# A transformer block's first MLP: block products by seven half-size ones, and one completion signal per weight unit

## The reference

```python
def squared_relu_mlp(h, w_in, w_out):
    return jnp.square(jax.nn.relu(h @ w_in)) @ w_out      # w_in 1024 x 4096, w_out 4096 x 1024
...
xl = xl + ml[5] * squared_relu_mlp(modulate(xl, norm_mlp_g[i], ml[3], ml[4]), w_mlp_in[i], w_mlp_out[i])
xc = xc + mc[5] * squared_relu_mlp(modulate(xc, norm_mlp_g[i], mc[3], mc[4]), w_mlp_in[i], w_mlp_out[i])
```

## Time and profile before

| what | value |
| --- | --- |
| median of 3 runs | 1614.97 us (1614.3 to 1968.04) |
| span of the profiled execution, first to last instruction | 1613.1 us |
| its instructions | 24225 |
| matmuls | 9440 |
| granted TensorE clock, 40 slices | nine tenths or more in each |
| HBM traffic | 100 GB/s over the span |

### The profile page before, as it was taken

One profiled execution on the slowest core, in us unless ns is written; L12 is line 12 of the kernel. 1 busy time (PEld: TensorE's weight loads), 2 busy tenths in 40 slices (PEclk: granted clock), 3 DMA queues, 4 the chain that ended last, 5 costly groups with the idle time before them and its releaser, 6 DMA issues.

```text
span 1613.1 us, 24225 instructions
## 1 busy us (share of the span) xinstructions
PE 1595.3 (99%) x9440; PEld 1433.7 (89%) x9440; DVE 983.8 (61%) x1315; ACT 517.5 (32%) x931; POOL 618.0 (38%) x402
## 2 busy tenths in 40 slices
PE   8999999999999999999999999999999999999998
PEld 5889988989999999999999888878889888888887
DVE  5697457258756764865784678229975825344364
ACT  4422466233211211211211512138864422222222
POOL 2422565335323322432331544244505644444441
PEclk9999999999999999999999999999999999999999
DMA  9473212213252234223332122110002322323221
GB/s 361 181 284 134 92 41 99 92 66 105 77 185 80 77 122 140 100 95 117 105 112 97 66 91 92 65 56 1 1 1 89 107 93 92 104 91 99 96 79 53
DMA packets 50334, 162.99 MB, mean 101 GB/s; under 512 B 6336, under 2 KB 8768, under 8 KB 46656
## 3 DMA queue, kind: packets, MB, share of 16 engines
q1 hardware_dynamic: 50240, 161.68, 29.1%
HBM read 158.78 MB, written 2.10 MB: 100 GB/s over the span
## 4 chain that ended last, share of the span: by engine, by line
PE 93%; DVE 3%; DMA 2%; issue 1%; ACT 1%; SPq 0%; POOL 0%; POOLq 0%; DVEq 0%; ACTq 0%
PE ps L1714 26%; PE ps L1715 26%; PE ps L1716 26%; PE ps L2259 3%; PE ps L2221 2%; PE ps L2248 1%; PE ps L2126 1%; PE ps L2114 1%; PE ps L2154 1%; PE ps L1938 1%; DMA mod_late<-w_mod_dram 1%; DMA mod_big<-w_mod_dram 1%; DVE h L1315 1%; DMA raw<-units_dram 1%; PE ps L2149 1%
## 5 line engine op out<-in xcount | busy, mean ns | idle before, releaser
L625 POOL TENSOR_TENSOR w_lo<-raw,w_hi 128x1024 fp32r<-128x1024 f32 (+1 forms) x235 | 483.6, 2070 | 837.9 <-ACT w_hi L784 837.7
L1714 PE MATMUL ps<-h,w_hi 128*128 128x384 f32 (+2 forms) x1176 | 409.8, 348 | 1.7 <-DVE h L1315 1.2
L1715 PE MATMUL ps<-h,w_lo 128*128 128x384 f32 (+2 forms) x1176 | 407.6, 347 | 0.0
L1716 PE MATMUL ps<-h,w_hi 128*128 128x384 f32 (+2 forms) x1176 | 407.3, 346 | 0.0
L784 ACT ACTIVATE w_hi<-raw 128x1024 fp32r<-128x1024 f32 x187 | 197.8, 1058 | 372.7 <-PE ps L1716 366.1
L1714 PE MATMUL ps<-hid_lo,w_hi 128*128 128x384 f32 (+2 forms) x800 | 277.6, 347 | 0.0
L1715 PE MATMUL ps<-hid_hi,w_lo 128*128 128x384 f32 (+2 forms) x800 | 276.6, 346 | 0.0
L1716 PE MATMUL ps<-hid_hi,w_hi 128*128 128x384 f32 (+2 forms) x800 | 276.4, 346 | 0.0
L1714 PEld LDWEIGHTS ps<-h,w_hi 128*128 128x128 f32 x1176 | 221.3, 188 | 25.2 <-issue 3.4
L1716 PEld LDWEIGHTS ps<-h,w_hi 128*128 128x128 f32 x1176 | 221.2, 188 | 16.4
L1715 PEld LDWEIGHTS ps<-h,w_lo 128*128 128x128 f32 x1176 | 221.4, 188 | 16.0
(11 more groups left out here) (237 smaller groups left out, 2268.9 us busy)
## 6 DMA issues: line engine op xcount, KB each, us to landing
raw<-units_dram SPq DMA_DIRECT2D x187, 512.0 KB, 3.3
mod_ring<-w_mod_dram SPq DMA_DIRECT2D x96, 256.0 KB, 3.3
mod_big<-w_mod_dram SPq DMA_DIRECT2D x16, 1024.0 KB, 10.2
mod_late<-w_mod_dram SPq DMA_DIRECT2D x8, 1024.0 KB, 7.9
xl<-x_dram SPq DMA_DIRECT2D x2, 2048.0 KB, 8.4
bias<-bias_dram SPq DMA_DIRECT2D x8, 384.0 KB, 3.7
xc<-ctx_dram SPq DMA_DIRECT2D x2, 1024.0 KB, 10.5
out_dram<-out_t SPq DMA_DIRECT2D x16, 128.0 KB, 1.9
```

What stands on the lines that cost most here:

```text
L625: ins = nc.gpsimd.tensor_tensor(w_lo[:, s, sl], raw[:, s, sl], w_hi[:, s, sl].bitcast(F32), op=ALU.subtract)
L1714: mm(out, a[0], b[1], start=start, stop=False)
L1715: mm(out, a[1], b[0], start=False, stop=False)
L1716: return mm(out, a[0], b[0], start=False, stop=stop)
```

## The change

The first MLP is cut into eight blocks (0 to 7) of 512 hidden columns. Block 0 does its first matrix as before (four units). In blocks 1 to 7 the product of a 1024 x 512 weight block and h is seen as a 2 x 2 matrix of halves (512 rows or 256 columns of the weights, 384 tokens), and computed with seven products of halves, 24 matmuls each, in place of eight (the Strassen-Winograd form). For it:

- four combinations of halves of h are made once, in block 0, by VectorE (`difference`, `less`, then `turn_high` on ScalarE and `turn_low` on VectorE): t1 replaces a quarter of h, t2, t3 and t4 are new tiles of 128 x 1536;
- four sums of weight quarters are made per block by GpSimd, so a block has four raw units but seven split ones in the first matrix;
- three of the four results are joined: ScalarE copies a partial product out of PSUM (`copy`), later products go on top of it in the same bank, and VectorE adds the copy (`joined`). The relu of three quarters is inside VectorE's square. The high part of the hidden layer is made by ScalarE, `quarter_high`.

The second matrix of blocks 0 to 5 has units of 512 x 256: two output tiles and four k-tiles each, in four banks (4 to 7), with one `unit_done` for both tiles, and every block adds all eight output tiles to the residual. Blocks 6 and 7 share one second matrix with whole units, as before. The chunks of `w_mod` are spread anew, up to two a block, and all loops of this stage are written out. The second layer's MLP is unchanged but for names. The core of the diff:

```diff
+BLOCKS = 8
+MOD_SEQ = [12, 16, 13, 17, 14, 18, 15, 19, 20, 21, 22, 23]
+MOD_OF = {b: [2 * b - 2, 2 * b - 1] for b in range(1, 6)} | {6: [10], 7: [11]}
...
+            for b in range(1, BLOCKS):
+                r, cs = M0 + block_raw(b) + 4, MOD_OF[b]
+                load_unit(r)
+                load_mod(cs[0], (4, 5))
+                load_unit(r + 1)
+                load_mod(cs[0], (6, 7))
+                load_unit(r + 2)
+                load_unit(r + 3)
...
+                    def outer_sums():
+                        raw_here(1)
+                        raw_here(3)
+                        if b == 1:
+                            pool.wait_ge(t_lo, 4)
+                        else:
+                            pool.wait_ge(lo_made, M0 + block_first(b - 1) + 4)
+                        nc.gpsimd.tensor_tensor(w_sum[:], a21, a22, op=ALU.add).then_inc(w_sums, 1)
+                        raw_here(0)
+                        pool.wait_ge(w_sums, n + 1)
+                        nc.gpsimd.tensor_tensor(a21, a11, a21, op=ALU.subtract).then_inc(w_sums, 1)
+
+                    if b < 7:
+                        outer_sums()
+                    low(w)
+                    if b == 7:
+                        outer_sums()
+                    pool.wait_ge(w_sums, n + 2)
+                    pool.wait_ge(lo_made, w + 1)
+                    nc.gpsimd.tensor_tensor(a11, w_sum[:], a11, op=ALU.subtract).then_inc(w_sums, 1)
+                    low(w + 1)
+                    raw_here(2)
+                    pool.wait_ge(w_sums, n + 3)
+                    pool.wait_ge(lo_made, w + 2)
+                    nc.gpsimd.tensor_tensor(w_sum[:], a12, a11, op=ALU.subtract).then_inc(w_sums, 1)
+                    for j in range(2, 11 if b < 6 else 7):
+                        low(w + j)
...
+                for i in range(4):
+                    u = M0 + i
+                    act.wait_ge(unit_done, u + 1)
+                    for bank, c0, n in both if i < 3 else even:
+                        ins = nc.scalar.activation(hidl_f[:, i, c0:c0 + n], ps[:, 2 * pair_of(u, i, True) + bank, 0:n],
+                                                   ACT.Relu)
+                    ins.then_inc(relu0_made, 1)
+                    high_u(u + 4)
+                    act.wait_ge(sq0_made, i + 1)
+                    nc.scalar.activation(hidh[:, i], hidl_f[:, i], ACT.Copy).then_inc(hq_hi, 1)
+                    if i == 1:
+                        turn_high(0, t3h[:], t3f[:])
+                    elif i == 2:
+                        turn_high(1, t2h[:], t2f[:])
+                        turn_high(2, t4h[:], t4f[:])
+                act.wait_ge(unit_done, M0 + 4)
+                turn_high(3, h_hi[:, 0:4, H1], t1f[:])
...
+                    high_sum(b, 3)
+                    copy(0, 0, 2)
+                    high_sum(b, 4)
+                    copy(1, 1, 1)
+                    high_u(w + 5)
+                    copy(0, 2, 0)
+                    high_u(w + 6)
+                    for q in range(4):
+                        if q == 3:
+                            copy(0, 6, 3, ACT.Relu)
+                        if b == 6 and q in (1, 2):
+                            high_sum(7, q)
+                        elif b != 6 or q == 0:
+                            high_u(w + 7 + q)
+                        quarter_high(q)
...
+                def difference(dst, spare, j0, tok0, j1, tok1):
+                    tt(dst, half_f(j0, 0, tok0), half_f(j1, 0, tok1), op=ALU.subtract).then_inc(dsteps, 1)
+                    st.n = st.n + 1
+                    st.wait(tt(spare, half_f(j0, 1, tok0), half_f(j1, 1, tok1), op=ALU.subtract))
+                    tt(dst, dst, spare, op=ALU.add).then_inc(tf_made, 1)
+
+                def less(dst, src, n, j, tok):
+                    dve.wait_ge(tf_made, n)
+                    st.wait(tt(dst, half_f(j, 0, tok), src, op=ALU.subtract))
+                    tt(dst, dst, half_f(j, 1, tok), op=ALU.add).then_inc(tf_made, 1)
...
+                difference(t1f[:], t4f[:], 0, H1, 0, H0)
+                first_square(0)
+                dve.wait_ge(tf_made, 1)
+                difference(t3f[:], t4f[:], 1, H1, 0, H1)
+                first_low(0)
+                less(t2f[:], t1f[:], 1, 1, H1)
+                first_square(1)
+                less(t4f[:], t2f[:], 3, 1, H0)
+                first_low(1)
+                turn_low(0, t3l[:], t3f[:], t3h[:])
+                first_square(2)
+                first_low(2)
+                turn_low(1, t2l[:], t2f[:], t2h[:])
+                turn_low(2, t4l[:], t4f[:], t4h[:])
+                first_square(3)
+                first_low(3)
+                turn_low(3, h_lo[:, 0:4, H1], t1f[:], h_hi[:, 0:4, H1])
...
+                def add_tile(b, m):
+                    w = M0 + block_first(b) + (7 if b else 4) + m // 2
+                    dve.wait_ge(unit_done, w + 1)
+                    add_pieces(0, 2 + m % 2, m, 5, xa(0, b, m))
...
+                    def joined(side, p, q):
+                        dve.wait_ge(unit_done, M0 + block_first(b) + p + 1)
+                        dve.wait_ge(s_copied, 4 * (b - 1) + (3, 2, 1)[q])
+                        src = quarter(b, q)[2]
+                        tt(src, part_ps(b, side), src, op=ALU.add).then_inc(s_added, 1)
+                        dve.wait_ge(s_added, 3 * (b - 1) + q + 1)
+                        square(q, 4 * b + q, src)
...
+                    steps(c, range(6))
+                    joined(1, 3, 0)
+                    steps(c, range(6, 7))
+                    low(0)
+                    joined(0, 4, 1)
+                    steps(c, range(7, 8))
+                    low(1)
+                    if b == 6:
+                        extract_late(c, 4)
+                    joined(1, 5, 2)
+                    low(2)
+                    dve.wait_ge(s_copied, 4 * b)
+                    square(3, 4 * b + 3, quarter(b, 3)[2])
+                    low(3)
+                    if b < 6:
+                        add_tile(b, 0)
+                        add_tile(b, 1)
+                        extract_late(c, 0)
+                        for m in range(2, 6):
+                            steps(c + 1, range(2 * m - 4, 2 * m - 2))
+                            add_tile(b, m)
+                        add_tile(b, 6)
+                        extract_late(c + 1, 0)
+                        add_tile(b, 7)
...
+                def second(b, before_tile):
+                    for n in range(4):
+                        u = M0 + block_first(b) + (7 if b else 4) + n
+                        s = u % SLOTS
+                        pe.wait_ge(lo_made, u + 1)
+                        for m, c in ((0, 1), (1, 1), (0, 0), (1, 0)) if n == 0 else ((0, 0), (0, 1), (1, 0), (1, 1)):
+                            tile = 2 * n + m
+                            if c == (n == 0):
+                                before_tile(tile)
+                            for k in range(4):
+                                if n == 0 and m == 0 and b == 0 and c:
+                                    pe.wait_ge(hq_made, k + 1)
+                                elif n == 0 and m == 0 and b and k % 2 == 0:
+                                    pe.wait_ge(hq_made, 4 * b + (1 if c else 3) + k // 2)
+                                w = slice(512 * m + P * k, 512 * m + P * k + P)
+                                cols = (H0, H1)[c]
+                                ins = three(ps[:, 4 + 2 * m + c, 0:EVEN], (w_hi[:, s, w], w_lo[:, s, w]),
+                                            (hidh[:, k, cols], hidl[:, k, cols]), k == 0, k == 3)
+                        ins.then_inc(unit_done, 1)
+
+                def before_second(b):
+                    def wait(tile):
+                        if b == 0 and tile == 0:
+                            pe.wait_ge(relu0_made, 4)
+                        elif b or tile > 1:
+                            pe.wait_ge(x_added, xa(0, b, tile) - 1)
+                        if tile == 2 and b:
+                            mod_mm(MOD_OF[b][0], 0)
+                        if tile == 7 and b:
+                            mod_mm(MOD_OF[b][1], 0)
+                    return wait
...
+                def product(b, p):
+                    u = M0 + block_first(b) + p
+                    s, bank = u % SLOTS, 2 * (p % 2) + (4 if b == 7 else 0)
+                    pe.wait_ge(lo_made, u + 1)
+                    if p in (2, 3, 4):
+                        pe.wait_ge(s_copied, 4 * (b - 1) + p - 1)
+                    elif p in (5, 6):
+                        pe.wait_ge(s_added, 3 * (b - 1) + p - 4)
+                    for m in range(2):
+                        for k in range(4):
+                            w = slice(512 * m + P * k, 512 * m + P * k + P)
+                            ins = three(ps[:, bank + m, 0:EVEN], (w_hi[:, s, w], w_lo[:, s, w]), operands[p](k),
+                                        k == 0 and p in (0, 1, 5), k == 3, onto=p in (2, 3, 4, 6))
```

(17 more changed lines are left out.)

435 lines of the change are left out of this document (300 added, 135 removed).

## The result

The changed kernel took 1766.1 us (median of 4 runs, 1753.1 to 1769.1) beside 1614.8 for the kernel before on the same chip (median of 4, one of which took 1968.04 us for a reason that is not known): a ratio of 1.092, interval 1.088 to 1.096. It is slower, as forecast, but by 151 us where 107 were forecast, and beyond the upper end of the range, 1752.

The account below looks back on a forecast made before the run. TensorE was taken to bound the kernel. A gain of 29.1 us from fewer matmuls against losses of 29.7, 27, 44, 15, 4 and 16 gave +106.6: 1721.6 us, 6.6% slower, range 1650 to 1752.

Parts of the forecast that it names:

- What bounds the kernel: Whole kernel: TensorE, busy 1595.3 of 1613.1 us, so each matmul removed saves its pitch and each wait costs its length.
- matmuls removed: First MLP: 168 fewer matmuls at 0.1733 us each, a gain of 29.1 us.
- A: Second matrix, blocks 0 to 5: one signal per two-tile unit makes TensorE wait at 18 boundaries, 1.65 us each, 29.7 us.
- B: Block 0: combinations of h delay the fourth relu and square; 25 us idle plus 2 us of clock, 27 us.
- C: Products of blocks 1 to 5: VectorE and GpSimd exclude each other on one port; queue walk gives 44 us lost.
- D: Second matrix: odd tiles' adds late, 3 us a block in blocks 1 to 5, 15 us; blocks 6 and 7, 4 us.
- E: Start of blocks 2 to 6: TensorE waits for a chunk's extraction behind tile 6's add, 3.2 us five times, 16 us.
- At nothing: First MLP's loads: no unit late enough to cost time; if cover went, up to 3.3 us per unit.
- The clock: Block 0's turn: slower clock after the long wait adds some 2 us, and changes only that term.
- Rival 3: First MLP: late sums delay weights and the clock falls after twelve waits, 1.7 us each; 1758 us, chance 0.16.
- Rival 1: First MLP: the port shared by VectorE and GpSimd costs nothing; 1652 us, chance 0.17.
- Rival 2: First MLP: work TensorE waits for is already done, so nothing is paid; 1586 us, chance 0.05.

Follow-up runs that it names:

- before_wait: The kernel before, made to wait at 24 tile boundaries of the first layer's MLP for the add of the tile just finished: 1652.9 us, ratio 1.024.
- tile_signal: The changed kernel with a second semaphore behind the even tile of each unit of the second matrix: 1684.1 us, ratio 1.043.
- keep_busy: The changed kernel with matmuls nobody reads put into nearly all of TensorE's waits in blocks 0 to 6: 1736.1 us, ratio 1.075.
- port_free: The changed kernel with GpSimd's low parts and nearly all weight sums of the first MLP cut to 32 of 1024 columns: 1657.7 us, ratio 1.026.

## Why the prediction was wrong in size

- **What bounds the kernel; matmuls removed: right.** 168 fewer; a wait that TensorE is given costs its whole length, and more.
- **A: right.** 1.41 to 1.45 us idle at each of 18 boundaries, 1.69 with the restart, against 1.65; `before_wait` has 1.61 for its somewhat shorter waits. The 0.08 for the way back stands in no row of the forecast; the trace shows 0.05, from an add's end at 612.22 to the matmul at 612.27. But as a price of the *signal* it was far too low, since `tile_signal` won 82 us.
- **B: right.** 20.2 idle before the fourth relu (21.8 forecast), then 2.97 (3.5). It restarted at 412.0, forecast 413.3.
- **C: mechanism right, size 44 against 29.5.** In block 1 to 4 the walk had 2.3, 4.0, 0.4 and 3.3; the trace of blocks 2 to 4 has 1.30, 1.83, 0.34 and 2.57. Block 1 lost 4.7 at two places and block 5 2.7 (4 forecast). I had taken the walk as it came, with a subtraction in the way at each place; in the trace it was there at some of them only. The sign that I named, squares with a mean near 2 us, did not come: the 15 of the first three quarters between 460 and 860 us have 1.26.
- **D: mechanism right, too small, 19 against 37.7.** The walk gave 5 a block, and I took 3, on the way to no meeting at all; it was 4.4. The `mod_mm` behind block 6's sixth product waited 10.7 us alone, over the end of 10 that I had set for both blocks.
- **E: right.** 3.65 us five times, 18.3 against 16.
- **At nothing: right.** No wait on a load or on `w_lo` is in TensorE's list in this stage.
- **The clock: this is the step that failed.** "It changes this term by those 2 us only" stood behind B, and nothing in A, C, D or E. The waits of 2.5 us and more were each followed by 3.1 to 6.0 us of TensorE's work at 1.2 GHz, and four of 1.8 us by 3.4: 41 us by TensorE's busy time, 40 by the record of the clock, at least 30 by `keep_busy`. Without them the terms as measured give 1613.1 - 29.1 + 140.8 = 1724.8 for the span, and the forecast was 1719.7. I had the row that shows it: 0.58 at 22 to 26 us, behind 4 us in which TensorE was busy 1.85. Those are 2.15 us of idle time in all, in waits of 0.82 and 1.33 us, no longer than the ones of C, D and E. I used it for the one wait of 20 us and not for the others. Rival 3, "it compounds", had this mechanism, twelve waits at 1.7; it was 22 at 1.8. Its 1758 is the nearest of all the forecasts, in part by luck: its other half, C at 60, did not come. What I set against it, nine tenths in each slice of before, says nothing about a kernel that has no such waits yet.

The Trainium skill (TensorE: Matmul & The Clock Gate, "HAM oscillation — how this bites in real kernels") prices the lower clock at half the time that TensorE spends at it. The rows agree nearly: a matmul of 0.32 us has 0.147 lost, 46%.

- **Rival 1, the port costs nothing: wrong, but priced nearly right.** With the port freed the kernel takes 1657.7; the rival's time was 1652. It is near in part by luck: the turn was shorter than its 20 (14.8), and some 14 us of half clock were not in it. (The run also has GpSimd's own work away, which the rival kept.)
- **Rival 2, the work is already behind it: wrong.** Not even `port_free` or `tile_signal` comes below the kernel before.

## What to carry to other kernels

A product that saves matmuls must not give TensorE waits. Price each wait by its length, plus 0.25 us for the restart, and look at the granted clock behind it: in this kernel 18 waits of 2.5 us and more cost another 1.9 us each on average, in stretches at half clock. Before adding elementwise work to VectorE and GpSimd, sum both engines' two-operand time over the stage: at 62 of 62.4 us none of the orders tried was free of waits. One added 10 us of them on the low parts, one took 15 away there and put 4.0 ahead of tile 7 in five blocks. And where a consumer's queue is in order, a completion signal that comes one tile earlier moves all that stands behind it: one semaphore here was worth 82 us, a quarter of it through the clock.

## What was not expected of the hardware

- In the changed kernel each of TensorE's 18 waits of 2.5 us and more was followed by a stretch at a granted clock of 0.50, in which it was busy for 3.1 to 6.0 us; in other runs some such waits were not, up to one of 3.65 us. The 24 waits of 0.9 to 1.5 us in `before_wait` left the mean clock at 0.999.
- Matmuls put into the waits keep the clock up, with the result unchanged: 30 us of 1766. Where they ended before the wait did, in blocks 2 to 4, a block took 85 us, what its matmuls, waits and restarts come to at full clock.
- The sum of many small collisions is not stable under reordering: the same work in four orders gave 23.3, 33.3, 8.2 and 25.5 us of waits on low parts.
